# A decoder block in float32: x and the final weight read again in pieces, PSUM additions ahead of a group's end, GpSimd weighs one output group

## The reference, cut to what matters

```python
xn = rmsnorm(h, norm_w[l], NORM_EPS)                   # h = x, one layer
(rq, rk, rv, rz, dq, dk, dv, dz, g_ret, g_diff) = jnp.split(xn @ w_in[l], SPLIT_POINTS, axis=-1)
o_ret  = rmsnorm(retention(rotary(rq), rotary(rk), rv)) * silu(rz)
o_diff = rmsnorm(diff_attention(rotary(dq), rotary(dk), dv, lam), subln_w) * 0.8 * silu(dz)
mixed  = sigmoid(g_ret) * (o_ret @ w_ret_up[l]) + sigmoid(g_diff) * (o_diff @ w_diff_up[l])
h      = h + mixed @ w_out[l]
return rmsnorm(h, final_norm_w, NORM_EPS)
```

## Time and profile before

| | |
|---|---|
| median of 3 runs (lowest, highest) | 1106.19 us (1106.04, 1106.44) |
| the profiled execution | 1109.03 us |
| its span, first to last instruction | 1106.8 us |
| mean granted TensorE clock | 0.993 of full speed |
| busy PE, PEld, DVE, ACT, POOL | 1082.7, 897.9, 749.7, 540.9, 46.7 us |
| the 16 DMA engines | 227.97 MB, 206 GB/s |
| rounding a unit on ACT, L686, x364 | 1060 ns of one |
| low part of a unit on DVE, L1025, x364 | 1243 ns of one |
| a unit of w_out from issue to landing, x32 | 512.0 KB, median 4.5 us |

### The profile page before, as it was taken

How to read it: one execution, slowest core, us unless ns; L and a number is a source line. 1 busy time by engine, 2 the same in 40 slices (tenths; PEclk the granted TensorE clock), 3 DMA queues, 4 the chain that set the end, 5 groups by cost and what they waited for, 6 DMA issues and landing times.

```text
span 1106.8 us, 13190 instructions
## 1 busy us (share of the span) xinstructions
PE 1082.7 (98%) x4864; PEld 897.9 (81%) x4864; DVE 749.7 (68%) x918; ACT 540.9 (49%) x695; POOL 46.7 (4%) x63
## 2 busy tenths in 40 slices
PE   9999999999999999999999999999999999999895
PEld 7888888888888887888888888888888888887674
DVE  6675575585566678767856776667667766676787
ACT  6644455344455544344644474446544654443453
POOL 0100000000000000000100010001000010000021
PEclk9999999999999999999999999999999999999898
DMA  9877667776666555677666757675667565676743
GB/s 330 293 239 218 176 197 203 206 205 198 192 204 193 188 191 171 199 237 211 190 202 199 223 173 213 189 238 168 212 198 229 172 218 199 201 235 201 257 150 117
DMA packets 132880, 227.97 MB, mean 206 GB/s; under 512 B 14416, under 2 KB 40784, under 8 KB 132048
## 3 DMA queue, kind: packets, MB, share of 16 engines
q1 hardware_dynamic: 132256, 223.98, 65.7%
q10 hardware_dynamic: 560, 3.15, 0.7%
HBM read 210.84 MB, written 2.10 MB: 192 GB/s over the span
## 4 chain that ended last, share of the span: by engine, by line
PE 90%; DVE 5%; DMA 2%; issue 1%; SPq 1%; ACT 1%; POOL 0%; POOLq 0%; ACTq 0%; DVEq 0%
PE bank L1491 25%; PE bank L1492 25%; PE bank L1493 25%; PE bank L1498 3%; PE bank L1499 3%; PE bank L1500 3%; DMA raw<-w_out_dram 1%; DVE w_lo L1025 1%; SPq L492 1%; PE bank L1560 1%; PE bank L1559 1%; PE bank L1558 1%; PE bank L1463 0%; DVE mixed L950 0%; DVE gate L1353 0%
## 5 line engine op out<-in xcount | busy, mean ns | idle before, releaser
L1025 DVE TENSOR_TENSOR w_lo<-raw,w_hi 128x1024 fp32r<-128x1024 f32 x364 | 450.6, 1243 | 312.5 <-ACT w_hi L686 312.0
L686 ACT ACTIVATE w_hi<-raw 128x1024 fp32r<-128x1024 f32 x364 | 385.6, 1060 | 482.1 <-PE bank L1493 415.1
L1491 PE MATMUL bank<-w_hi,xt_hi 128*128 128x512 f32 x1136 | 443.3, 390 | 0.0
L1493 PE MATMUL bank<-w_hi,xt_lo 128*128 128x512 f32 x1136 | 442.1, 389 | 0.0
L1492 PE MATMUL bank<-w_lo,xt_hi 128*128 128x512 f32 x1136 | 442.0, 389 | 0.0
L1493 PEld LDWEIGHTS bank<-w_hi,xt_lo 128*128 128x128 f32 x1136 | 213.2, 188 | 44.6
L1491 PEld LDWEIGHTS bank<-w_hi,xt_hi 128*128 128x128 f32 x1136 | 213.3, 188 | 43.8
L1492 PEld LDWEIGHTS bank<-w_lo,xt_hi 128*128 128x128 f32 x1136 | 213.3, 188 | 43.6
L1498 PE MATMUL bank<-w_hi,xt_hi 128*128 128x512 f32 x104 | 42.6, 409 | 8.5 <-DVE w_lo L1025 7.5
L1491 PE MATMUL bank<-w_hi,ot_hi 128*128 128x512 f32 x128 | 49.8, 389 | 0.0
L1492 PE MATMUL bank<-w_lo,ot_hi 128*128 128x512 f32 x128 | 49.8, 389 | 0.0
(11 more groups left out here) (182 smaller groups left out, 861.1 us busy)
## 6 DMA issues: line engine op xcount, KB each, us to landing
raw<-w_in_dram SPq DMA_DIRECT2D x284, 512.0 KB, 4.3
raw<-w_ret_up_dram SPq DMA_DIRECT2D x32, 512.0 KB, 4.4
raw<-w_diff_up_dram SPq DMA_DIRECT2D x32, 512.0 KB, 4.6
raw<-w_out_dram SPq DMA_DIRECT2D x32, 512.0 KB, 4.5
rot<-squares_t SPq DMA_DIRECT2D x96, 64.0 KB, 2.4
zs<-squares_t SPq DMA_DIRECT2D x48, 64.0 KB, 2.2
normed<-squares_t SPq DMA_DIRECT2D x48, 64.0 KB, 2.2
raw<-w_in_dram SPq DMA_DIRECT2D x8, 256.0 KB, 5.4
```

The source lines that it names most:

```text
L686: act.activation(w_hi[:, s, :, :], raw[:, s, :, :], ACT.Copy).then_inc(hi_ready, 1)
L1025: dve.tensor_tensor(w_lo[:, s, :, :], raw[:, s, :, :], w_hi[:, s, :, :].bitcast(F32), ALU.subtract) \
L1491: pe.matmul(bank[bk][:, :], hi, w_hi[:, s, kk, :], start=k == 0, stop=False)
L1493: return pe.matmul(bank[bk][:, :], lo, w_hi[:, s, kk, :], start=False, stop=k == KT - 1)
```

## The change

1. x and the final weight are sent for by SP instead of ACT. The weight (one transfer of 1024 KB) stands behind unit U_TAIL + 9; x comes in four transfers of 512 columns of both token blocks (512 KB each) behind units U_TAIL + 20, 28, 36 and 44, each with a wait for `mixed_ready` of its columns. `x_again` becomes two semaphores, one for each pair group, and the weight has its own.
2. In both pair products the first three banks are added at step s % 16 = 14, one step earlier than the first two before, and the fourth at step 15. For w_out this concerns its first group; the last one is done behind the loop as before.
3. POOL weighs only group 2. In group 3 DVE does both of a block's parts with the weight in the operation; ACT scales columns 0 to 1023, DVE does 1024 to 2047. The stores wait for `y_early` (ACT's two) and `y_late` (DVE's two).

```diff
@@ SP @@
                     load_unit(weight[name], n, u, col)
+                    if n == U_TAIL + 9:
+                        for b in range(BLOCKS):
+                            sp.wait_ge(drained[6 + b], diff_uses_high(DIFF_ITS, 0))
+                        sp.dma_start(final_w, final_norm_w.rearrange("(a n) -> a n", a=1).broadcast_to([P, D])) \
+                          .then_inc(final_w_landed, 16)
+                    if n > U_TAIL + 12 and (n - U_TAIL - 12) % UNITS == 0 and (n - U_TAIL - 12) // UNITS <= GROUPS_D:
+                        j = (n - U_TAIL - 12) // UNITS - 1
+                        sp.wait_ge(mixed_ready, 2 * (j + 1))
+                        cols = slice(j * COLS, (j + 1) * COLS)
+                        sp.dma_start(gate[:, :, cols], x.rearrange("(b p) n -> p b n", p=P)[:, :, cols]).then_inc(x_again[j // 2], 16)
...
             for b in range(BLOCKS):
                 for i in range(GROUPS_D // 2):
-                    sp.wait_ge(y_even, b * (GROUPS_D // 2) + i + 1)
-                    sp.wait_ge(y_odd, b * (GROUPS_D // 2) + i + 1)
+                    sp.wait_ge((y_early, y_late)[i], 2 * (b + 1))
@@ POOL @@
-            pool.wait_ge(x_again, 32)
+            pool.wait_ge(final_w_landed, 16)
             for e in range(SUMS):
                 weigh(e)
             for b in range(BLOCKS):
-                weigh(SUMS + 2 * b)
                 pool.wait_ge(h_row_step[b], 4)
@@ ACT, scale_h @@
-                act.wait_ge(h_weighted, SUMS + 1 + b)
+                act.wait_ge(h_weighted, SUMS)
                 act.wait_ge(h_row_step[b], 5)
-                for c in (1, 3):
+                for c in (0, 1):
                     y = mixed[:, b, c * COLS:(c + 1) * COLS]
-                    act.activation(y, y, ACT.Copy, scale=h_rstd[:, b:b + 1]).then_inc(y_odd, 1)
+                    act.activation(y, y, ACT.Copy, scale=h_rstd[:, b:b + 1]).then_inc(y_early, 1)
...
-                if g == GROUPS_D and u == 5:
-
-                    act.wait_ge(mixed_ready, 2 * GROUPS_D)
-                    act.dma_start(gate[:, :, :], x.rearrange("(b p) n -> p b n", p=P)).then_inc(x_again, 16)
-                    act.dma_start(final_w, final_norm_w.rearrange("(a n) -> a n", a=1).broadcast_to([P, D])) \
-                       .then_inc(x_again, 16)
@@ DVE @@
-                if s % KT in (KT - 1, 0):
-                    for i in range(2):
-                        merge_ret((s - 1) // KT, 2 * (s % KT == 0) + i)
+                if s % KT == KT - 2:
+                    for i in range(SUMS - 1):
+                        merge_ret(s // KT, i)
+                if s % KT == KT - 1:
+                    merge_ret(s // KT, SUMS - 1)
...
-                    dve.wait_ge(x_again, 32)
+                    dve.wait_ge(x_again[group - PAIR_GROUPS], 16 * 2)
...
-                if out_s in (KT - 1, KT):
-                    for i in range(2):
-                        add_own(PAIR_GROUPS, 2 * (out_s - (KT - 1)) + i)
+                if out_s == KT - 2:
+                    for i in range(SUMS - 1):
+                        add_own(PAIR_GROUPS, i)
+                if out_s == KT - 1:
+                    add_own(PAIR_GROUPS, SUMS - 1)
@@ DVE, scale_h @@
-                if b == 0:
-                    dve.wait_ge(h_weighted, SUMS)
+                dve.wait_ge(final_w_landed, 16)
                 dve.wait_ge(h_row_step[b], 5)
-                y = mixed[:, b, 0:COLS]
-                cols = slice(j * COLS, (j + 1) * COLS)
-                dve.tensor_scalar(y, y, h_rstd[:, b:b + 1], None, ALU.mult).then_inc(y_even, 1)
-                dve.scalar_tensor_tensor(out=mixed[:, b, cols], in0=gate[:, b, cols], scalar=h_rstd[:, b:b + 1],
-                                         in1=final_w[:, cols], op0=ALU.mult, op1=ALU.mult).then_inc(y_even, 1)
+                for c in (j, j + 1):
+                    cols = slice(c * COLS, (c + 1) * COLS)
+                    dve.scalar_tensor_tensor(out=mixed[:, b, cols], in0=gate[:, b, cols], scalar=h_rstd[:, b:b + 1],
+                                             in1=final_w[:, cols], op0=ALU.mult, op1=ALU.mult).then_inc(y_late, 1)
```

More of the change, by code:

```diff
@@ L338, in build @@
         mt_hi_ready = sem("mt_hi_ready")
-        x_again = sem("x_again")
+        x_again = [sem(f"x_again{p}") for p in range(PAIR_GROUPS)]
+        final_w_landed = sem("final_w_landed")
         h_ready = sem("h_ready")
@@ L344, in build @@
         h_row_step = [sem("h_row_step0"), sem("h_row_step1")]
-        y_even = sem("y_even")
-        y_odd = sem("y_odd")
+        y_late = sem("y_late")
+        y_early = sem("y_early")
         stored = sem("stored")
```

## The result

| | before | after |
|---|---|---|
| median (lowest, highest), 4 runs each | 1106.24 us (1106.04, 1106.44) | 1098.47 us (1098.27, 1098.85) |
| the profiled execution | 1109.03 us | 1098.85 us |
| its span | 1106.8 us | 1097.0 us |
| from PE's last matmul to the end of the span | 11.9 us | 10.9 us |

What follows compares the result with a forecast made beforehand. TensorE, busy 1082.7 of 1106.8 us, was taken as the bound, leaving its gaps, end and low clock to win. Gains 6.2 + 2.6 + 1.2 + 1.7 = 11.7 us off 1106.19 gave 1094.5 us; 8-in-10 range 1091 to 1099.

Steps and rivals of the forecast that it cites:

- the clock's rival: Unit 9 of w_out: a 3.7 us wait drops the clock, 2.9 us paid again, 1098.3 us; chance 0.07.
- a clock of 0.50 behind it: Sign of being wrong: granted clock at half level behind PE's remaining wait at unit 9 of w_out.
- w_ret_up, 2.6 us: Second pair group of w_ret_up: earlier bank additions remove both PE waits, gain 2.6 us (1.6 to 2.6).
- The wait at unit 9, 6.2 us: Unit 9 of w_out: reload in pieces cuts the 9.0 us loss to 2.8, gain 6.2 (5.3 to 7.4).
- As the clock held 5.4 us of idle, it holds this one, and the 2.9 us are not paid: Unit 9 of w_out: the remaining wait brings no low clock, so its earlier 2.9 us cost goes.
- 5.7 were taken: Landing time in us of the last of three raw transfers ahead of unit 9, from a similar burst's median.
- w_out's second group, 1.2 us: Second pair group of w_out: earlier bank additions recover part of 3.0 us lost, gain 1.2 (0.3 to 3.0).
- The 1.8 us forecast for the wait that remains: Unit 3 of w_out's second group: PE's wait goes from 1.6 to about 1.8 us.
- The end, 1.7 us: Behind the last matmul: last value 0.1 to 0.5 us earlier, stores gain more; gain 1.7 (0.7 to 2.7).
- The pieces, cost 0: Pieces of x and final weight where they now stand in SyncE's queue: cost 0, at most 1 us.

Runs made afterwards that it cites:

- b_merges: Kernel before the change with only w_ret_up's bank additions and gate multiplications moved earlier: 1103.49 us against 1106.73.
- c_adds: Kernel before the change with only the bank additions of w_out's first group moved earlier, GpSimd weighing as before: 1104.79 us against 1106.73.
- d_tail: Kernel before the change with only the new end (POOL's two weighings, the four scalings, the stores): 1104.85 us against 1106.73.
- a_reload: Kernel before the change with only x and the final weight sent in pieces from SyncE's queue: 1104.65 us against 1106.73.
- l: j, but x and the final weight loaded as before the change, from ScalarE's queue: 1095.51 us.
- e_act_turns: Changed kernel with the last eight turn DMAs issued by ScalarE instead of SyncE: 1099.49 us.
- g: Changed kernel with ScalarE issuing the last eight turns, DVE splitting units 3 and 9 before the sums, and GpSimd weighing later: 1096.93 us.
- h_late_weigh: Changed kernel with GpSimd's four weighings started only after unit 13 of w_out's second group is split: 1098.34 us.
- i: Changed kernel with the third and fourth piece of x sent behind units 12 and 20 of w_out instead of 4 and 12: 1098.42 us.
- j: Changed kernel with DVE splitting units 3 and 9 before the sums and GpSimd weighing after unit 13: 1092.43 us against 1106.83.

## Why the prediction was right, and where it was off

The direction was right and 1098.47 lies inside 1091 to 1099, near its upper end, since 3.9 of the 11.7 us didn't come. It lies outside the 1092 to 1097.5 that the prediction gave its own mechanism: what kept it inside is that the range reached into the clock's rival. One of the prediction's signs of being wrong came, "a clock of 0.50 behind it".

- **w_ret_up, 2.6 us: right.** Both waits are gone; b_merges alone gave 3.0 us (2.0 to 4.0).
- **The wait at unit 9, 6.2 us: the step that failed is "As the clock held 5.4 us of idle, it holds this one, and the 2.9 us are not paid".** What came before was right within its bounds. The last transfer of the burst took 6.27 us where 5.7 were taken, between the ends 4.5 and 6.6 (the chain of waits of the changed kernel):

```profile
1011.03 6.27 DMA raw<-w_out_dram
1017.30 0.03 issue
...
1017.39 1.24 DVE mixed L953
```

  So 3.4 us were lost for 2.8. But the clock fell about 2 us into the idle and stayed low until 1026.5; that cost 2.7 us, and the gain was 2.9. One fall in one trace had been taken as a measure of how long the clock bears an idle, and it isn't one. All traces together (idle of PE in w_ret_up and w_out, and what was lost beyond the wait where the low clock followed):

| idle of PE | waits | followed by the low clock | lost beyond the wait |
|---|---|---|---|
| 5.6 to 6.1 us (before, b, c, d) | 4 | 4 | 1.6 to 2.9 us |
| 4.0 to 4.4 us (a, l) | 2 | 2 | 3.0, 1.7 us |
| 3.2 to 3.5 us (the change, e, g, h, i) | 5 | 5 | 1.7 to 2.7 us |
| 1.0 to 2.6 us | 18 | 1 (c_adds, 1.77 us) | 1.7 us |

  It fell within the idle or up to 1.4 us behind it (e_act_turns). The rival "the clock falls all the same" had 0.07 and gave 1098.3; it is what happened, and by these traces it was the likely case. Each row counts one execution of a kernel, and none has an idle between 2.6 and 3.2 us.
- **w_out's second group, 1.2 us: right, 1.6.** One wait is left, for the reason given: three of four weighings meet DVE's operations with two SBUF inputs. h_late_weigh shows it, since these take 1.22 and 0.69 us again once the weighings are gone. The 1.8 us forecast for the wait that remains were 1.4.
- **The end, 1.7 us: 1.0.** The first store starts 3.3 us behind the last matmul instead of 5.0, as forecast, and square_half takes 0.42. But the last value came no more than 0.2 us sooner. ScalarE's chain of scaling, square and DVE's mean behind it sets the second rstd, as the prediction had it, and brought POOL's power 0.6 us sooner. Then the power took longer:

```profile
1089.84 0.21 DVE L1417 TENSOR_SCALAR h_ms<-h_ss,h_more 128x1 f32<-128x1 f32 x1 [1.12 <-ACT junk L908]
1089.97 2.73 DVE L1426 SCALAR_TENSOR_TENSOR mixed<-gate,h_rstd,zs 128x512 f32<-128x512 f32 x4
```

```profile
1090.13 0.99 POOL L646 TENSOR_TENSOR h_rstd<-h_ms,minus_half 128x1 f32<-128x1 f32 x1 [2.22 <-DVE h_ms L1417]
```

  0.99 us, where the power of the first block, with DVE not at two SBUF inputs, took 0.55, and before's second one 0.72. The last store starts 6.9 us behind the last matmul in both kernels. The last two stores follow within 0.8 us, so the queue isn't empty for the last one, and it lands in 3.7 us, not in the least, 2.6. The 1.0 us come from its issue (0.45 us for 1.00) and a landing 0.4 us shorter. The term was mis-sized by counting the sooner first store and an emptier queue in full. By its times d_tail gained 1.8 us (0.9 to 2.8), of which its trace shows 1.0 at the end.
- **The pieces, cost 0:** nothing waits in w_diff_up. The 0.4 us more at units 4 to 8 aren't shown to be theirs.

## What to carry to other kernels

A wait that stays behind is worth more than its length when TensorE's clock may fall in it. When a trace shows a long idle, look at the clock behind it as well as in it: here all eleven waits of 3.25 us and more were followed by the low clock, at 1.6 to 3.0 us each, and of eighteen between 1.0 and 2.6 us one was. Ask of each instruction on a critical engine whether what it waits for is needed by what stands behind it; the split of unit 9 stood behind sums that waited for units 10 and 11. With the weighings moved away, changing the two gave some 6 us (h to j), where spreading x and the weight gave 3.1 (l to j). Moving a transfer to another queue doesn't make it land sooner by itself: the turns went from 2.2 to 5.2 us when they ran beside what they had been ahead of.

## What was not expected of the hardware

- The granted clock fell 5.2 us after PE's stop in one execution and 2 us after it in another, and it fell with 1.77 us of idle and not with 2.52. It came back 3.2 us (d_tail) to 6.2 us (a_reload) after the restart. Its state in the first 10 us differed between executions by 2 us of time.
- A transfer of 64 KB in small pieces, issued from ScalarE beside three of 512 KB, took 5.2 us to land, and 2.2 from SyncE ahead of them; the three took 6.0 and 5.5 (medians).
- On POOL a power of 128x1 took 0.55 us and, next to DVE's operations with two SBUF inputs, 0.99, in each of the ten traces with the new end.
